# The PEER expert mixer of a two-layer decoder step: gathered expert rows replaced by a dense pass over all 16384 experts

## The chip, the cores and the metric

One Trainium2 chip (trn2), one core. The metric is the device time of one execution in microseconds; the median of three runs is the number that counts. The profile is that of one execution, taken by the hardware profiler.

## The reference

One inference step for 256 prompt tokens and 8 sample tokens (264 columns in all), D = 1024, everything in float32. Layer 0 mixes by a gated linear recurrence, layer 1 by latent attention over a paged cache; both layers end in the same expert mixer, which is what the change is about:

```python
q = (xb @ w_q).reshape(blk, PEER_HEADS, PEER_KEY_DIM)            # 8 heads
s1 = einsum('thd,hnd->thn', q[..., :half], k1)                   # 128 keys each
s2 = einsum('thd,hnd->thn', q[..., half:], k2)
v1, i1 = top_k(s1, 16); v2, i2 = top_k(s2, 16)
sv, si = top_k(all 256 sums v1 + v2, 16)
e = 128 * i1 + i2 at si                                          # of 16384 experts
gate = softmax(sv)
act = gelu(einsum('thkd,td->thk', u[e], xb), approximate=False)
y = einsum('thk,thkd->td', gate * act, v[e])
```

u and v are tables of 16384 x 1024 for each layer (67 MB each). Then x = LayerNorm(alpha * x + y).

## The kernel before, in words

Five engine programs are written out by hand and meet through semaphores (TensorE `pe`, ScalarE `act`, VectorE `dve`, GpSimd `pool`, and SyncE `sp`, which only issues transfers). The tokens lie in three tiles: two of 128 prompt tokens and one of 8 samples. `xT` holds x transposed, 8 blocks of 128 x 264. The program runs in stages: the recurrence (`*_hgrn`, 8 heads, `project` on L327 with 32 matmuls of 128 x 264 per head), join and normalisation (`pe_join` L646, `dve_ln` L670 to L685), the first mixer, attention (`*_mla`: prompt first, then the paged cache of each sample), join and normalisation, the second mixer, a last normalisation.

The mixer (`sp_peer`, `pool_peer`, `pe_peer`, `act_peer`, `dve_parts`) loops over the 8 heads, two per pass. For a head, TensorE computes the queries of all tokens (L919) and the scores (L927). VectorE chooses 16 of each half list and 16 of the 256 sums (`top16`, L1050 to L1060), looks up the indices by one-hot products over 16 x 16 (L1088 to L1092) and writes them to `idx`. POOL then gathers, for each tile and each of the 16 choices, one row of u per token into an eight-slot ring (L817, 512 KB), and the same of v. VectorE takes the dot product of every gathered u row with x (L1125, 512 in all); ScalarE applies Gelu and turns each column of weights into a 128 x 128 diagonal (L1021); TensorE multiplies it with the gathered v rows, so that they add up in PSUM (L944):

```python
for k in ks:
    after(pe, "pe", v_land[k % RING], 16 * (4 * hg + 2 * t + k // RING + 1))
    after(pe, "pe", dg_ready, 32 * hg + 16 * t + k + 1)
    for c in range(2):
        mm = pe.matmul(ybank(t, c, P), dg[:, k % 4, :], vring[:, k % RING, 512 * c:512 * c + 512], ...)
    mm.then_inc(v_free, 1)
```

The 8 samples are repacked so that their 128 choices fill one gather each of u and v (`repack` L935, `unpack_s`, L982). L944 therefore runs 2 layers x 8 heads x 2 tiles x 16 choices x 2 halves times. A head's routing runs one head ahead. The first head's routing of each layer is done apart and early (`pe_first`, `act_first`, L875 to L897): in layer 1, two of its three tiles lie inside attention, ahead of the page loop. In the first mixer a normalised tile is handed on while the next still adds up (L971, L977).

What the prediction also touches: `level_decays` (L474, L475) runs on VectorE and POOL at the same time, and L487 is a product of 1024 elements on POOL; L516 is a VectorE product with a pointer scalar; L1001 is ScalarE's copy of 264 columns out of PSUM; L1322 is the first matmul of attention.

## Time and profile before

| | |
|---|---|
| median of three runs | 2455.47 us (2450.78 to 2457.2) |
| span of the profiled execution | 2712.4 us, the only time shown for it |
| TensorE busy, matmul | 1916.9 us (71%), 6209 records |
| TensorE weight loads | 989.2 us, beside the matmuls |
| VectorE busy | 1398.3 us (52%) |
| ScalarE busy | 572.2 us (21%) |
| POOL busy | 1216.3 us (45%) |
| DMA | 642.5 MB, mean 237 GB/s |
| chain that ended last | PE 49%, issue 20%, VectorE 9% |

The span runs from the first to the last instruction of one profiled execution; it is 257 us longer than the median of the runs without the profiler. Busy is the union of an engine's instructions in the span. The granted clock is the share of TensorE's full 2.4 GHz; its other level is half of that, 1.2 GHz, and a mean between them says for how much of a stretch each held. A window row has its stretch and length first, then the busy time (and the number of records) of TensorE's matmuls, its weight loads, VectorE, ScalarE and POOL, then the clock, the DMA engines' busy share and GB/s.

### The profile page before, as it was taken

To read this page: it belongs to the slowest core of one execution; us is meant where nothing else is said; L and a number is where in the kernel's file an instruction comes from. 1 tells how busy PE (TensorE), PEld (TensorE's weight loads), DVE (VectorE), ACT (ScalarE), POOL (GpSimd) and SP (SyncE) were. 2 spreads that over 40 slices of the span, in tenths; PEclk is the share of its full clock that TensorE was granted. 3 is DMA by queue.
4 is the path that set the end of the run, shared out by engine and by line. 5 is a ranking of instruction groups with operands and counts; after the bars stand their busy time and mean duration, and the time that the engine had idled before them with its cause. 6 is when DMAs were issued, how large, how long until landed. Compare 5 with 4: busy or idle time off the path is not lost.

```text
span 2712.4 us, 28807 instructions
## 1 busy us (share of the span) xinstructions
PE 1916.9 (71%) x6209; PEld 989.2 (36%) x6209; DVE 1398.3 (52%) x3767; ACT 572.2 (21%) x1295; POOL 1216.3 (45%) x1229
## 2 busy tenths in 40 slices
PE   6997877556573847558887899877657484656657
PEld 5775343223332323223454444334223232223222
DVE  3554475664565656463252422347646555645563
ACT  3343021112121211122231333112212121111212
POOL 1110055764654657565002132435655465646464
PEclk9988878787786969779998999879778797877779
DMA  7530198996968869697303132468987788969596
GB/s 222 133 97 27 54 336 302 328 347 243 347 250 299 310 250 348 252 367 269 153 11 96 31 88 72 162 222 300 347 326 254 275 296 319 356 222 360 213 344 247
DMA packets 254991, 642.53 MB, mean 237 GB/s; under 512 B 23401, under 2 KB 115074, under 8 KB 254610
## 3 DMA queue, kind: packets, MB, share of 16 engines
q0 software_dynamic: 156160, 555.82, 56.1%
q1 hardware_dynamic: 98706, 85.37, 10.4%
q8 instruction: 38, 0.62, 0.1%
q14 instruction: 87, 0.71, 0.1%
HBM read 635.00 MB, written 6.10 MB: 236 GB/s over the span
## 4 chain that ended last, share of the span: by engine, by line
PE 49%; issue 20%; DVE 9%; another core or an unknown queue 7%; DMA 4%; ACT 4%; DVEq 3%; POOL 2%; PEldq 0%; ACTq 0%; SPq 0%; POOLq 0%; PEld 0%
PE bank L944 26%; DMA arena<-in_peer_v,idx 3%; PE bank L646 3%; PE bank L1447 2%; PE bank L1468 2%; POOL arena L817 2%; PE bank L919 2%; PE bank L338 1%; DVEq L476 1%; PE bank L327 1%; DMA arena<-in_peer_u,idx 1%; PE bank L1322 1%; PE bank L927 1%; PE bank L1349 1%
## 5 line engine op out<-in xcount | busy, mean ns | idle before, releaser
L944 PE MATMUL bank<-arena,dg 128*128 128x512 f32 x2048 | 974.8, 636 | 291.3 <-ACT dg L1021 153.9
L1125 DVE SCALAR_TENSOR_TENSOR arena<-arena,x 128x1024 f32<-128x1024 f32 x512 | 616.6, 1225 | 361.3 <-DMA arena<-in_peer_u,idx 323.7
L817 POOL DMA_INDIRECT arena<-in_peer_v,idx x512 | 531.1, 1037 | 597.2 <-DVE arena L1125 244.9
L944 PEld LDWEIGHTS bank<-arena,dg 128*128 128x128 f32 x2048 | 410.7, 205 | 843.1 <-issue 842.8
L817 POOL DMA_INDIRECT arena<-in_peer_u,idx x512 | 553.3, 1081 | 320.5 <-issue 260.3
L1021 ACT ACTIVATE dg<-cst,w 128x128 f32<-128x128 f32 x512 | 194.6, 399 | 759.6 <-PE bank L944 475.9
L919 PE MATMUL bank<-xT,wbig 128*128 128x264 f32 x448 | 116.7, 422 | 110.2 <-issue 110.2
L1311 POOL DMA_DIRECT2D arena<-in_cache_kpe x80 | 42.8, 536 | 275.9 <-issue 275.9
L919 PEld LDWEIGHTS bank<-xT,wbig 128*128 128x128 f32 x448 | 92.7, 211 | 129.9 <-issue 112.7
L927 PE MATMUL bank<-g_all 128*128 128x128 f32 (+1 forms) x168 | 36.6, 381 | 132.5 <-issue 106.6
L1104 DVE RECIPROCAL gsum_s<-gsum_s 8x1 f32<-8x1 f32 x16 | 2.4, 151 | 235.1 <-ACT rp L1010 207.0
L327 PE MATMUL bank<-xT,arena 128*128 128x264 f32 x512 | 117.0, 390 | 2.0 <-DMA arena<-in_hgrn_w_in 2.0
L327 PEld LDWEIGHTS bank<-xT,arena 128*128 128x128 f32 x512 | 97.8, 192 | 18.7 <-issue 2.0
L474 POOL TENSOR_TENSOR scratch<-scratch 128x128 f32<-128x128 f32 x16 | 7.0, 439 | 200.1 <-DVEq L523 200.1
L646 PE MATMUL bank<-wbig,xT 128*128 128x512 f32 (+1 forms) x192 | 91.0, 630 | 0.0
L935 PE MATMUL bank<-rp,cst 8*128 8x32 f32 x32 | 8.8, 362 | 114.2 <-DVE rp L1106 64.2
L927 PEld LDWEIGHTS bank<-g_all 128*128 128x128 f32 (+1 forms) x168 | 26.2, 223 | 142.7 <-issue 140.9
L1447 PE MATMUL bank<-arena,qst 128*16 128x512 f32 x128 | 60.4, 594 | 9.9 <-DVEq L1722 9.5
L1736 DVE COPY scratch<-bank 16x512 f32<-16x512 f32 x32 | 21.7, 679 | 85.6 <-PE bank L1448 85.4
L998 ACT ACTIVATE g_all<-bank 128x256 f32<-128x256 f32 x14 | 5.4, 383 | 242.4 <-remote 123.4
L1311 POOL DMA_DIRECT2D scratch<-in_cache_kpe x48 | 25.6, 534 | 66.8 <-issue 66.8
L646 PEld LDWEIGHTS bank<-wbig,xT 128*128 128x128 f32 (+1 forms) x192 | 31.4, 165 | 60.3 <-issue 60.3
(317 smaller groups left out, 2271.6 us busy)
## 6 DMA issues: line engine op xcount, KB each, us to landing
arena<-in_hgrn_w_in SPq DMA_DIRECT2D x32, 512.0 KB, 7.0
wbig<-in_peer_w_q SPq DMA_DIRECT2D x14, 1024.0 KB
arena<-in_cache_ckv SPq DMA_DIRECT2D x80, 128.0 KB, 2.0
arena<-in_peer_u,idx POOLq DMA_INDIRECT x512
arena<-in_peer_v,idx POOLq DMA_INDIRECT x512
scratch<-in_cache_ckv SPq DMA_DIRECT2D x48, 128.0 KB, 2.0
arena<-in_state_hgrn SPq DMA_DIRECT2D x8, 512.0 KB, 7.1
wbig<-in_hgrn_w_out SPq DMA_DIRECT2D x1, 4096.0 KB, 15.6
```

The lines of the kernel that those rows point to most:

```text
L327: mm = pe.matmul(bank[g % 2][:, 0:NT], wh[j][:, k, c, :], xT[:, k, :], start=(k == 0), stop=(k == KO - 1))
L338: mm = pe.matmul(bank[4 + l // 2][:, (l % 2) * 256 + t * P:(l % 2) * 256 + (t + 1) * P], left, right, start=True, stop=True)
L646: mm = pe.matmul(ybank(t, c, nt), xT[:, k, t0:t0 + nt], wbig[:, k, cols], start=False, stop=(k == KO - 1))
L817: pool.indirect_dma_start(out=dst, out_offset=None, in_=table, in_offset=bass.IndirectOffsetOnAxis(ap=rows, axis=0)).then_inc(done, 16)
L919: mm = pe.matmul(b[:, 0:NT], wq[j][:, k, s * P:(s + 1) * P], xT[:, k, :], start=(k == 0), stop=(k == KO - 1))
L927: mm = pe.matmul(b[0:nt, s * P:(s + 1) * P], qT[:, s, t0:t0 + nt], kT[:, s, :], start=True, stop=True)
L944: mm = pe.matmul(ybank(t, c, P), dg[:, k % 4, :], vring[:, k % RING, 512 * c:512 * c + 512], start=False, stop=False, skip_group_check=True)
L1021: act.activation(dg[:, k % 4, :], ident, ACT.Copy, scale=w[t][:, k:k + 1]).then_inc(dg_ready, 1)
L1125: dve.scalar_tensor_tensor(uring[:, k % RING, :], uring[:, k % RING, :], 1.0, x[:, t, :], ALU.mult, ALU.mult, accum_out=dots[t][:, k:k + 1 ...
L1311: eng.dma_start(buf[(b + 1) % 3][:, bass.ds(g, 1), :].rearrange("p a l -> p (a l)"), cache[page]).then_inc(landed[(b + 1) % 3], 16)
L1447: pe.matmul(out, qst[:, c, :], cT[:, q % 2, c, :], start=(c == 0), stop=False)
L1468: pe.matmul(out, dpT[:, pg, :], cbuf[slot][:, pg, :], start=(pg == 0), stop=False)
```

## The change

The gathers go. Each mixer streams its tables once, in tiles of 128 x 1024 (512 KB) through a ring of six: 16 tiles of w_q, 128 of u, 128 of v (`NSTREAM` = 272). The host lays the tables out so that a tile is contiguous. The program is unrolled.

- Queries: tile n of w_q against `xT` gives half a head's queries for all 264 tokens (`project`); scores follow for each head; those of the samples of all heads are computed at once from zero-padded queries (`zq`).
- VectorE does all routing of the layer in one go (`choose`, `indices`, `gates`): 8 heads for tile 0, then for tile 1, then the 64 rows of the samples. The results are a first key, a second key and a gate for every choice; TensorE turns them (`turn_table`) so that `tab` has choices on the partitions and tokens on the columns.
- Dense u: tile i (first key i, 128 second keys) against `xT`: 8 matmuls of 128 x 264 give the dots of 128 experts with all tokens. ScalarE writes their Gelu to row block H[:, i, :], 264 columns. H fills `big` (128 x 264 x 4 bytes on each partition), which also holds the former `scratch`, `arena` and `wbig`; the routing's buffers lie where rows 70 and above go.
- Gate map: from tile 62 (`FRONT`) on, each tile comes with one chunk of 4 tokens, 66 chunks in all. For a token, `hot2` (one-hot of the second key: POOL squares the distance, ScalarE takes relu(1 - d)) times `hot1` (one-hot of the first key times the gate, VectorE) sums the 128 choices to a 128 x 128 map of gates. VectorE multiplies it into the rows of H that are there (`use_gates`), ScalarE stores the others (`keep_gates`), and each later tile is multiplied in when its Gelu is ready (`gate_tile`).
- Dense v: tile i against H[:, i, :], 8 matmuls of 128 x 264, one for each PSUM bank, summed over all 128 tiles. VectorE adds alpha * xT, and TensorE turns the sum back for the normalisation, all three tiles after the last v tile.
- In attention, the first routings between the joins and the page loop go; `rt`, `qlT`, `olT`, `dpT` move into `shared`. Attention's weights w_dkv, w_dq, w_uq and w_ukv are loaded within the first layer's v tiles.

The diff, cut to its core:

```diff
-RING = 8
+RING = 6
+NSTREAM = 2 * HH + 2 * NKEYS
+NCHUNK = NT // 4
+FRONT = 62
+LAG = 1
+NTMP = NKEYS - (FRONT - LAG)
+TAB_AT = (56, 61)
...
+        big = sb("big", [P, NKEYS * NT])
+        scratch = big[:, 0:SCRATCH]
+        arena = big[:, SCRATCH:SCRATCH + 16384]
+        wbig = big[:, SCRATCH + 16384:].rearrange("p (k n) -> p k n", k=KO)
...
+        H = big[:, :].rearrange("p (i t) -> p i t", t=NT)
...
-            def gather(dst, table, rows, done):
-                pool.indirect_dma_start(out=dst, out_offset=None, in_=table,
-                                        in_offset=bass.IndirectOffsetOnAxis(ap=rows, axis=0)).then_inc(done, 16)
...
+            def stream(n):
+                m = NSTREAM * l + n
+                if m >= RING:
+                    sp.wait_ge(tile_done, m - RING + 1)
+                if n < 2 * HH:
+                    src = peer_w_q[l, n]
+                elif n < NA:
+                    src = peer_u[l, n - 2 * HH]
+                else:
+                    src = peer_v[l, n - NA]
+                dst = ring[:, m % RING, :]
+                if n < NA:
+                    dst = dst.rearrange("p (k n) -> p k n", k=KO)
+                sp.dma_start(dst, src).then_inc(land[m % RING], 16)
...
+            def project(n):
+                w = landed(n)
+                if n >= 4:
+                    pe.wait_ge(dps_taken, NA * l + n - 3)
+                for k in range(KO):
+                    mm = pe.matmul(bank[n % 4][:, 0:NT], w[:, k * P:(k + 1) * P], xT[:, k, :],
+                                   start=(k == 0), stop=(k == KO - 1))
+                mm.then_inc(tile_done, 1)
...
+            def gate_map(c):
+                if c == 0:
+                    pe.wait_ge(sc_ready, (HH + 1) * (l + 1))
+                    pe.wait_ge(tab_ready, 3 * (l + 1))
+                if c >= 4:
+                    pe.wait_ge(gate_kept, NCHUNK * l + c - 3)
+                pe.wait_ge(hot2_ready, NCHUNK * l + c + 1)
+                pe.wait_ge(hot1_ready, NCHUNK * l + c + 1)
+                for j in range(4):
+                    mm = pe.matmul(bank[4 + c % 4][:, j * P:(j + 1) * P], hot2[c % 2][:, j, :], hot1[c % 2][:, j, :],
+                                   start=True, stop=True)
+                mm.then_inc(gate_ready, 1)
...
+            for i in range(NKEYS):
+                if i == TAB_AT[0]:
+                    turn_table(0)
+                if i == TAB_AT[1]:
+                    turn_table(1)
+                if i == FRONT:
+                    turn_table(2)
+                if i >= FRONT:
+                    gate_map(i - FRONT)
+                project(2 * HH + i)
+                if i == 1:
+                    scores(HH - 1)
+                    sample_scores()
+            pe.wait_ge(gate_used, NCHUNK * (l + 1))
+            pe.wait_ge(gate_kept, NCHUNK * (l + 1))
+            for i in range(NKEYS):
+                w = landed(NA + i)
+                if i == FRONT - LAG:
+                    pe.wait_ge(tile_gated, NTMP * (l + 1))
+                for k in (4, 5, 6, 7, 0, 1, 2, 3):
+                    if i == 0 and k == 0:
+                        pe.wait_ge(dps_taken, NA * (l + 1))
+                    mm = pe.matmul(bank[k][:, 0:NT], w[:, k * P:(k + 1) * P], H[:, i, :],
+                                   start=(i == 0), stop=(i == NKEYS - 1))
+                mm.then_inc(tile_done, 1)
...
+            def act_tile(i):
+                act.wait_ge(tile_done, NSTREAM * l + 2 * HH + i + 1)
+                b = bank[(2 * HH + i) % 4]
+                n, j = gated(i), i - (FRONT - LAG)
+                if n:
+                    if j >= 3:
+                        act.wait_ge(tile_gated, NTMP * l + j - 2)
+                    ins = act.activation(tmp[j % 3][:, 0:n], b[:, 0:n], ACT.Gelu)
+                if n < NT:
+                    ins = act.activation(H[:, i, n:NT], b[:, n:NT], ACT.Gelu)
+                ins.then_inc(dps_taken, 1)
...
+            for c in range(NCHUNK):
+                keep_gates(c)
+                if c + 2 < NCHUNK:
+                    make_hot2(c + 2)
+                act_tile(FRONT + c)
...
+            for c in range(NCHUNK):
+                pool.wait_ge(tab_ready, 3 * l + chunk_tile(c) + 1)
+                if c >= 2:
+                    pool.wait_ge(hot2_ready, NCHUNK * l + c - 1)
+                d = dist[c % 2]
+                pool.tensor_tensor(d, bc(places, 1, 4), bc(tab[:, 1, 4 * c:4 * c + 4], 2, P), ALU.subtract)
+                pool.drain()
+                pool.tensor_tensor(d, d, d, ALU.mult).then_inc(dist_ready, 1)
...
+            def make_hot1(c):
+                dve.wait_ge(tab_ready, 3 * l + chunk_tile(c) + 1)
+                if c >= 2:
+                    dve.wait_ge(gate_ready, NCHUNK * l + c - 1)
+                for j in range(4):
+                    t = 4 * c + j
+                    ins = dve.tensor_scalar(hot1[c % 2][:, j, :], places, tab[:, 0, t:t + 1], tab[:, 2, t:t + 1],
+                                            ALU.is_equal, ALU.mult)
+                ins.then_inc(hot1_ready, 1)
...
+            def use_gates(c):
+                f = FRONT - LAG + c
+                dve.wait_ge(gate_ready, NCHUNK * l + c + 1)
+                dve.wait_ge(dps_taken, NA * l + 2 * HH + f)
+                h = H[:, 0:f, 4 * c:4 * c + 4].rearrange("p i t -> p t i")
+                dve.tensor_tensor(h, h, bank[4 + c % 4][:, :].rearrange("p (t i) -> p t i", t=4)[:, :, 0:f],
+                                  ALU.mult).then_inc(gate_used, 1)
+
+            def gate_tile(i):
+                n, j = gated(i), i - (FRONT - LAG)
+                dve.wait_ge(dps_taken, NA * l + 2 * HH + i + 1)
+                dve.wait_ge(gate_kept, NCHUNK * l + n // 4)
+                dve.tensor_tensor(H[:, i, 0:n], H[:, i, 0:n], tmp[j % 3][:, 0:n], ALU.mult).then_inc(tile_gated, 1)
...
+            make_hot1(0)
+            make_hot1(1)
+            for c in range(NCHUNK):
+                use_gates(c)
+                if c + 2 < NCHUNK:
+                    make_hot1(c + 2)
+                if c:
+                    gate_tile(FRONT - LAG + c - 1)
+            gate_tile(NKEYS - 2)
+            gate_tile(NKEYS - 1)
+            for k in range(KO):
+                dve.wait_ge(tile_done, NSTREAM * (l + 1))
+                dve.scalar_tensor_tensor(xT[:, k, :], xT[:, k, :], ALPHA, bank[k][:, 0:NT],
+                                         ALU.mult, ALU.add).then_inc(acc_taken, 1)
```

What moves on the engines. TensorE (`ring` is the stream's ring, `big` holds H and the routing's buffers, `arena` the gathered rows, `dg` the diagonals, `rp` the samples' choices), at the start of the first mixer, before:

```order
L944 MATMUL bank<-arena,dg 128x512 x16
L935 MATMUL bank<-rp,cst 128x32
L944 MATMUL bank<-arena,dg 128x512 x16
L914 MATMUL bank<-cst,wbig 128x128 x2
L919 MATMUL bank<-xT,wbig 128x264 x16
L927 MATMUL bank<-g_all 128x128 x4
L927 MATMUL bank<-g_all 8x128 x2
L944 MATMUL bank<-arena,dg 128x512 x32
L982 MATMUL bank<-wbig,wmask 8x512 x2
```

and now, from the samples' scores to the first chunk of the gate map:

```order
L827 MATMUL bank<-kT,big 64x128 x16
L806 MATMUL bank<-xT,ring 128x264 x432
L836 MATMUL bank<-cst,big 128x128 x3
L806 MATMUL bank<-xT,ring 128x264 x40
L836 MATMUL bank<-cst,big 128x128 x3
L806 MATMUL bank<-xT,ring 128x264 x8
L838 MATMUL bank<-cst,big 128x8 x3
L850 MATMUL bank<-x 128x128 x4
L806 MATMUL bank<-xT,ring 128x264 x8
```

The 512-column products with diagonals are gone, and runs of 264-column products stand in their place, eight to a tile; behind L838 the pair L850 and L806 repeats 66 times, and L882 follows with 1024 of them in one run.

VectorE in the chunk phase now (`shared` holds the turned table and three Gelu tiles, `x` the one-hots, `bank` the gate map):

```order
L1068 TENSOR_TENSOR big<-big,bank 128x4x66
L1059 TENSOR_SCALAR x<-cst,shared 128x128 x4
L1075 TENSOR_TENSOR big<-big,shared 128x20
L1068 TENSOR_TENSOR big<-big,bank 128x4x67
L1059 TENSOR_SCALAR x<-cst,shared 128x128 x4
```

In each chunk the product with the map grows by one row of H, the four one-hots stay, and the tile's own product grows by 4 columns up to 264; the dot products of 1024 elements that stood here before are gone.

## Rows read from the trace of the kernel before

**Rows 1.** The page: the span and the bytes
```profile
span 2712.4 us, 28807 instructions
...
HBM read 635.00 MB, written 6.10 MB: 236 GB/s over the span
```

**Rows 2.** Windows: busy PE, PEld, DVE, ACT, POOL; granted clock, DMA share, GB/s
```profile
0.00:337.00 337.00, 275.87 (x1275) 201.32 (x1276) 166.50 (x476) 101.84 (x213) 32.30 (x49) 0.89 0.38 105
337.00:1285.00 948.00, 610.47 (x1503) 289.89 (x1501) 541.40 (x1437) 170.21 (x415) 557.09 (x525) 0.80 0.83 305
...
1293.00:1773.00 480.00, 419.33 (x1974) 212.37 (x1974) 167.35 (x463) 129.91 (x254) 96.95 (x152) 0.94 0.28 91
1773.00:2701.00 928.00, 605.80 (x1442) 284.14 (x1442) 507.59 (x1362) 168.46 (x408) 530.01 (x504) 0.81 0.81 295
...
575.00:595.00 20.00, 12.28 (x38) 6.00 (x36) 16.67 (x27) 0.19 (x1) 15.43 (x16) 0.90 1.01 403
1600.00:1680.00 80.00, 75.91 (x382) 32.20 (x381) 20.90 (x60) 28.14 (x45) 24.05 (x45) 1.00 0.30 85
103.00:117.00 14.00, 14.00 (x65) 11.98 (x64) 10.97 (x30) 7.09 (x13) 3.62 (x5) 1.00 0.39 92
```

**Rows 3.** Groups of instructions: TensorE's matmuls on L944 and L327
```profile
L944 PE MATMUL bank<-arena,dg 128*128 128x512 f32 x2048 | 974.8, 636 | 291.3 <-ACT dg L1021 153.9 <-issue 111.0 <-DMA arena<-in_peer_v,idx 26.2
L327 PE MATMUL bank<-xT,arena 128*128 128x264 f32 x512 | 117.0, 390 | 2.0 <-DMA arena<-in_hgrn_w_in 2.0
```

**Rows 4.** Timeline of TensorE in a recurrence head: start us, us, instructions merged
```profile
101.22 1.95 PE L338 MATMUL bank<-scratch 128*128 128x128 f32 x16
103.01 14.41 PE L327 MATMUL bank<-xT,arena 128*128 128x264 f32 x64
```

**Rows 5.** Timeline: TensorE and VectorE as the first mixer starts
```profile
314.75 0.66 PE L875 MATMUL bank<-cst,keys_first 128*128 128x128 f32 x2 [2.41 <-ACT xT L631]
...
322.10 0.66 PE L623 MATMUL bank<-cst,o_all 8*128 8x8 f32 x8 [0.47 <-ACT g_all L897]
...
340.76 1.28 DVE L670 BATCH_NORM_STATS2 stats<-bank 8x6 f32<-8x512 f32 x2 [8.91 <-issue]
```

**Rows 6.** Timeline of VectorE: normalisations behind the first mixer
```profile
1285.66 1.30 DVE L670 BATCH_NORM_STATS2 stats<-bank 128x6 f32<-128x512 f32 x2 [3.27 <-PEq L977]
...
1290.30 1.28 DVE L670 BATCH_NORM_STATS2 stats<-bank 8x6 f32<-8x512 f32 x2
```

**Rows 7.** Timeline of TensorE in attention: the second mixer's first routings
```profile
1491.77 0.51 PE L875 MATMUL bank<-cst,keys_first 128*128 128x128 f32 x2 [2.52 <-ACT xT L631]
...
1505.46 0.71 PE L883 MATMUL bank<-g_all 128*128 128x128 f32 x4 [0.47 <-ACT g_all L893]
```

**Rows 8.** Timeline of VectorE over one choice of 16; groups by form
```profile
322.19 0.49 DVE L1050 MAX8 v<-g_all 128x8 f32<-128x128 f32 x2 [6.14 <-ACT g_all L897]
...
327.88 0.42 DVE L1060 FIND_INDEX8 si<-sv,cand 128x8 uint32<-128x256 f32 x1
...
L1090 DVE TENSOR_TENSOR oh<-oh,i12f 128x512 f32<-128x512 f32 x32 | 22.2, 692 | 2.4
...
L593 DVE TENSOR_TENSOR o_all<-o_all,rstd 128x1024 f32<-128x1024 f32 x2 | 2.5, 1226 | 0.2
```

**Rows 9.** Timeline of VectorE and of POOL in the first head
```profile
30.06 0.28 DVE L475 TENSOR_TENSOR scratch<-scratch 128x128 f32<-128x128 f32 x1
30.27 1.98 DVE L474 TENSOR_TENSOR scratch<-scratch 128x128 f32<-128x128 f32 x1
...
29.15 0.44 POOL L475 TENSOR_TENSOR scratch<-scratch 128x128 f32<-128x128 f32 x1
30.12 1.98 POOL L487 TENSOR_TENSOR arena<-arena,scratch 128x1024 f32<-128x1024 f32 x1 [0.53 <-issue]
```

**Rows 10.** Groups by form: a VectorE and a ScalarE instruction over 264 columns
```profile
L516 DVE TENSOR_SCALAR arena<-arena,omlb 128x264 f32<-128x264 f32 x8 | 2.9, 358 | 15.1 <-ACT arena L412 12.5 <-issue 2.6
...
L1001 ACT ACTIVATE g_all<-bank 128x264 f32<-128x264 f32 x28 | 10.4, 389 | 194.2 <-remote 151.9 <-PE bank L919 32.0 <-issue 10.3
```

More of the change, by code:

```diff
@@ L1055, in top16 @@
                 dve.drain()
-                for v_, i_, src, tmp in rows:
-                    dve.max(v_[:, 8:16], tmp)
+                for v_, i_, src, rest in rows:
+                    dve.max(v_[:, 8:16], rest)
                 dve.drain()
-                for v_, i_, src, tmp in rows:
-                    dve.max_index(i_[:, 8:16], v_[:, 8:16], tmp)
-            def route(hg, t, j, first=False):
-                nt = TILES[t][1]
-                after(dve, "dve", rs_taken, 6 * hg + (2 * t + 2 if first else 4 + t))
-                top16(*[(v12[0:nt, s, :], i12[0:nt, s, :], sc[0:nt, t, s, :], sc2[0:nt, s, :]) for s in range(2)])
+                for v_, i_, src, rest in rows:
+                    dve.max_index(i_[:, 8:16], v_[:, 8:16], rest)
@@ new lines, in dve_peer @@
+            NR = NS * HH
+            for h in range(HH):
+                dve.wait_ge(sc_ready, (HH + 1) * l + h + 1)
+                choose(h, P, sc[:, 0, h, :])
+            differences(P, HH, gex[0])
+            indices(P, HH, picked[0][:, 0:2, :].rearrange("p s (h k) -> p (s h) k", h=HH))
+            for h in range(HH):
+                choose(h, P, sc[:, 1, h, :])
+            gates(0, P, HH, gex[0], picked[0][:, 2, :].rearrange("p (h k) -> p h k", h=HH))
+            dve.sem_inc(picked_ready, 1)
@@ L1292, in sp_mla, with load_pages @@
             sp_ln(sp, 2)
-            load_pages(sp, cbuf, cache_ckv, page_in, lambda: sp_first(sp, 1))
-        def load_pages(eng, buf, cache, landed, between=None):
+            load_pages(sp, cbuf, cache_ckv, page_in)
+        def load_pages(eng, buf, cache, landed):
             eng.wait_ge(ptab_in, 16)
@@ L1301, in load_pages @@
             for b in range(NS):
-                if b == 2 and between:
-                    between()
                 if b == 1:
@@ L1728, in dve_mla @@
             dve_ln(dve, 2, (0, 1))
-            route, dot, weigh, heads = dve_parts(dve, 1)
-            for t in range(2):
-                route(HH, t, 0, True)
             def take_scores(b, q):
```

704 lines of the change are left out of this document (265 added, 439 removed).

## The prediction

> **What bounds the kernel now.** I read the stretches first, then the costliest groups, then the timeline at the borders of the two expert mixers. The stretches [rows 2] divide the span of 2712.4 us [rows 1]: 337 us of recurrence and joins, the first mixer up to 1285, attention from 1293 to 1773, the second mixer up to 2701, and a tail of 11. So the mixers hold 948 + 928 = 1876 us. In both the DMA share is above 0.8 at about 300 GB/s, TensorE is busy for only two thirds, and its granted clock is 0.80 and 0.81 of the full one. A stretch of gathers alone reaches 403 GB/s at share 1.01 [rows 2]. The mixers are paced by gathered rows, and in the gaps TensorE falls to its lower level of 1.2 GHz.
>
> The decisive row is of another kind. The program has 2 x 8 x 2 x 16 x 2 = 1024 matmuls on L944, and the trace has 2048 [rows 3]; it has 256 on L327, and the trace has 512. **An f32 matmul is two records**, and its cost is twice the step from one record to the next. That step stands in an unbroken run of L327 with just the shape that the change uses, 128x128 weights against 264 columns: 64 records, 14.41 us, the last lasting 0.386, so (14.41 - 0.39) / 63 = 0.2225 us at clock 1.00 [rows 2, 4]. One such matmul costs 0.445 us. For 128 columns the step is (1.95 - 0.27) / 15 = 0.112 us, a matmul 0.224 [rows 4].
>
> **The sum, part by part.**
> A tile of the stream (512 KB) feeds 8 matmuls of 264 columns: 3.56 us. A mixer has 16 tiles of w_q, 128 of u and 128 of v: 272 x 3.56 = 968.3 us. The one-hot products are 66 chunks x 4 matmuls x 0.224 = 59.1 us. Key scores: 32 matmuls, 7.2 us, and 16 for the samples, 3.6 us. Three turned tables, about 1.3. At the first chunk TensorE must wait for the last table to go through ScalarE (0.3) and to become a one-hot (0.6), about 1.5; the cold start costs about 2. Together **1043 us per mixer** where 948 and 928 stand now.
>
> What else runs in these 1043 us should hide behind TensorE:
> - Transfers: 512 KB in 3.56 us is 147 GB/s against 403 reached [rows 2], with five tiles in flight, 17.8 us of lead. The 7 MB of attention weights that SP now puts into the v tiles fit in the same margin. Without that cover the stream would cost 524 KB / 403 GB/s = 1.3 us per tile.
> - Routing on VectorE: one choice of 16 from two lists takes from 322.19 to 328.30, 6.1 us [rows 8]; 17 of them, 104 us. The index look-up for 8 heads has three passes over 4096 elements; from 512 and 1024 elements (0.69 and 1.23 us, 1.04 ns each more) a pass is 4.4 us, with its small operations 15 us, twice. With gates and samples and a start at 16 us it ends near 157 us. The third table is due at tile 78, after 78 x 3.56 + 11 = 289 us. There are 130 us to spare.
> - ScalarE: one or two Gelu reads per tile, 0.39 us each [rows 10]; in the chunk phase a 512-element one-hot and the kept gates besides, about 1.6 us of 4.46.
> - The chunk phase is the tight one. TensorE needs 3.56 + 0.90 = 4.46 us per chunk. VectorE: a product over 244 to 504 elements (0.42 to 0.69), four TENSOR_SCALAR of 128 (each at most the 0.36 of 264 columns), a product of up to 264 (0.42): 2.4 us. POOL: two products of 512 elements; between 0.44 for 128 and 1.98 for 1024 [rows 9] that is 1.1 each, 2.2 us. Side by side nothing is late. In turns they make 4.6 us, 0.1 above TensorE.
>
> What is removed: all gathers, the 512 dot products of 1.2 us, the diagonals, the per-head routing. None of it lies on the new path, so it is not subtracted again; it is the 1876 us that I replace. POOL's queue loses its gathers, and SP's queue only gains transfers with room around them.
>
> The rest moves little:
> - Start of the first mixer: TensorE no longer inserts the first routing at 314.75. The sample tile's turn and join, 322.10 to 340.76 (18.7 us) [rows 5], begin at about 313.5, end at 332, and with the normalisation (4.6, the distance of two BATCH_NORM rows [rows 6]) and the turn the mixer starts at **338**.
> - End of a mixer: now the tiles are normalised while others still accumulate. Later all come at once: eight reads of the sum 3, transposes 1, three normalisations 13.7, a turn 1: **18.5 us** before L1322 may start; at the very end **20** with the output.
> - Attention: 1293 to 1773, less the two first routings between 1490 and 1506 [rows 7], 15 us: **465**.
>
> Sum against the profile: 338 + 1043 + 18.5 + 465 + 1043 + 20 = **2927 us**, against the span of 2712.4.
>
> The runs of before have a median of 2455.5 us, 257 less than this profiled span. So profiling lengthens something, and no row says what. The TensorE part cannot shrink: 264 columns at 0.2225 us are the full 2.4 GHz with two cycles per column. I let only the other 842 us shrink: by nothing at one end, at the other by the whole 9.5% (80 us). Since the excess most likely sits in the transfer-bound mixers, which are gone, I take 4%, 32 us. That gives **2895 us** for a run, 18% slower.
>
> **Rules weighed.** POOL and VectorE do hinder each other: beside POOL's 1024-element product of 1.98 us a VectorE product of 128 elements took 1.98 instead of 0.28 [rows 9]. The Trainium skill (SBUF — State Buffer, Who interferes with whom) says the same: the shared port pair is an exclusive lock, and a VectorE instruction with two SBUF inputs, or in a two-port mode, waits for the whole GpSimd instruction. By that rule the chunk is the 4.6 us in turns, and my sum would be 2 x 66 x 0.14 = 18 us longer.
> The widest stride of a row here is 8 elements (no cost seen); the change reads H at a stride of 264. The same page (the note on cachelines in The DMA port swizzle) says that each access which crosses into a new 16-byte line pays a penalty, without a figure.
>
> **The rivals.**
> A. *The tile costs half, and the smaller traffic wins.* If a matmul were one record of 0.2225 us, a mixer would be 272 x 1.78 + 36 (half of the 71 us of one-hots, scores and tables) + 7 for starts and waits = 527 us were nothing else late. The chunk phase would then be paced by POOL and VectorE, up to 4.6 us for each of the 66 chunks in place of 2.2, so 527 to 680, and the run 810 + 2 x (527 to 680), 1865 to 2170: faster. For it: DMA is the bound now, and bytes fall from 635 MB [rows 1] to about 360. Against it: both counts in rows 3. The point from which it decides: 440 us lie between 2895 and 2455, over 2 x 2176 matmuls 0.10 each, so from 0.34 us per matmul downwards. Chance 0.03.
> B. *The chunk phase is bound by VectorE and POOL.* If strided products cost double (+0.5) and each locked operation loses a hand-over (five of 0.1), the chunk is 5.6 us, 1.1 above TensorE: 132 x 1.1 = 150 us, a run of 3045. It decides as soon as the two in turns pass 4.46 us. Chance 0.10.
> C. *Profiling lengthens everything alike.* 2927 x 0.905 = 2650 us. Against it: the full-clock step in rows 4. Still slower. Chance 0.06.
> D. *The clock does not hold for a millisecond of dense work.* From 1600 to 1680 TensorE was busy for 95% with clock 1.00 [rows 2], and the lower level appears here behind waits. Each per cent is 21 us; above 3100. Chance 0.03.
>
> **How the numbers follow.** Forecast as argued, 2820 to 2970: 0.77. A 0.03, B 0.10, C 0.06, D 0.03, and 0.01 for landing within 0.3% of before by a mix of A and the rest. The range takes the forecast's bounds (842 us shrunk by 80 at the low end, rounding the unknown ends down to 2820; the lock's 18 us and half of B at the high end): 2820 to 3000. A measurement can tell 0.3%, 7 us, from no change. Faster 0.03, same 0.01, slower 0.96.
>
> **What would show it.** Right: two records per matmul on the new lines of 264 columns, a step of 0.2225, granted clock 1.00 through both mixers, TensorE busy above 95% there, DMA near 150 GB/s, two mixers of about 1043 us. In the chunk phase TensorE's waits on the one-hots near zero. Wrong: gaps of TensorE behind VectorE or POOL of over 0.5 us per chunk (B), a clock below 0.95 in the dense tiles (D), tiles of 1.8 us (A), or a run more than 100 us below its own profile (C).

## The result and the profile after

The changed kernel takes **2930.9 us** (median of 4 runs, 2927.8 to 2931.6) against 2456.3 us of the kernel before (four runs, 2450.8 to 2468.1): ratio 1.193, interval 1.189 to 1.197, slower. Its profiled run took 2927.84 us with a span of 2926.2, so here profile and runs agree within 0.2%. One thing has to be known for all that follows: the kernel before takes 2451 to 2468 us on some chips and 2617 to 2722 on others, as the experiments show; where a ratio stands, it is against runs of the kernel before on that experiment's own chip, and since these scatter by 3% on the slower kind, a ratio there moves by 1% with the runs that it is taken against.

The page of the changed kernel, its busy times, slices, transfers and the chain that ended last (they answer to [rows 1] and to the page's chain of before):

```profile
span 2926.2 us, 36735 instructions
PE 2778.4 (95%) x13193; PEld 2205.2 (75%) x13193; DVE 851.2 (29%) x2583; ACT 512.6 (18%) x1231; POOL 381.1 (13%) x439
...
PE   7987999999999999999787998899999999999997
...
PEclk9987999999999999999898999999999999999999
...
DMA packets 160321, 357.89 MB, mean 122 GB/s; under 512 B 14473, under 2 KB 85666, under 8 KB 159666
...
PE 90%; DVE 3%; DVEq 2%; ACT 2%; issue 1%; SPq 0%; ACTq 0%; DMA 0%
```

Traffic fell from 643 to 358 MB and DMA is 0% of the chain; TensorE is 90% of it. The windows cut at the borders of the stages (first mixer, its tail, attention, second mixer, end, and the first mixer's chunk phase) answer to [rows 2]. The columns after the stretch are its length, then each engine's busy time, PEclk, DMA share and GB/s:

```profile
core 0: us, PE busy (x) PEld busy (x) DVE busy (x) ACT busy (x) POOL busy (x), PEclk, DMA share, GB/s
339.50:1383.30 1043.80, 1042.62 (x4988) 899.32 (x4988) 263.89 (x857) 139.72 (x380) 140.91 (x132) 1.00 0.47 143
1383.30:1399.20 15.90, 4.17 (x33) 3.24 (x33) 14.38 (x31) 1.84 (x5) 0.00 (x0) 0.79 0.80 284
1399.20:1863.90 464.70, 410.54 (x1900) 203.82 (x1900) 131.09 (x360) 127.91 (x248) 69.55 (x129) 0.94 0.18 51
1863.90:2906.60 1042.70, 1041.59 (x4988) 898.68 (x4988) 263.85 (x856) 139.70 (x380) 140.58 (x132) 1.00 0.45 136
2906.60:2926.20 19.60, 3.07 (x25) 2.38 (x24) 15.74 (x32) 0.88 (x3) 0.00 (x0) 0.71 0.14 55
633.40:923.70 290.30, 290.30 (x1567) 256.52 (x1568) 134.22 (x385) 89.42 (x259) 136.41 (x128) 1.00 0.39 118
```

TensorE is busy for 1042.6 of 1043.8 us of the first mixer, at clock 1.00. The chunk phase from the first to the last one-hot product has no gap at all, with VectorE at 134 and POOL at 136 of 290 us. So the time is the number of TensorE's records times their step. The groups of that chunk phase, busy time and mean of one, then idle time before them and its releaser:

```profile
L806 PE MATMUL bank<-xT,ring 128*128 128x264 f32 x1040 | 242.2, 386 | 0.0
L1059 DVE TENSOR_SCALAR x<-cst,shared 128x128 f32<-128x128 f32 x256 | 72.6, 347 | 0.0
L988 POOL TENSOR_TENSOR x<-cst,shared 128x512 f32<-128x512 f32 x64 | 70.0, 1094 | 149.9 <-ACT x L940 149.9
L850 PE MATMUL bank<-x 128*128 128x128 f32 x527 | 69.5, 275 | 1.1 <-ACT x L940 1.1
L990 POOL TENSOR_TENSOR x<-x 128x512 f32<-128x512 f32 x64 | 66.6, 1041 | 9.1
L1068 DVE TENSOR_TENSOR big<-big,bank 128x244 f32<-128x244 f32 (+32 forms) x65 | 54.3, 835 | 164.3 <-PE bank L850 164.3
```

L850 has waited 1.1 us in 66 chunks. The two lines of 264-column products over the whole run, and the v tiles of the first mixer in one piece of TensorE's timeline (start, length, records):

```profile
L806 PE MATMUL bank<-xT,ring 128*128 128x264 f32 x4608 | 1055.1, 387 | 0.6 <-ACT xT L624 0.6
L882 PE MATMUL bank<-big,ring 128*128 128x264 f32 x4096 | 911.7, 386 | 0.0
...
927.39 455.84 PE L882 MATMUL bank<-big,ring 128*128 128x264 f32 x2048
```

These are two records for each of the 2304 and 2048 products of the program, and the step from one record to the next is (455.84 - 0.39) / 2047 = 0.2225 us.

Where the time went: outside the mixers 339.5 + 15.9 + 464.7 + 19.6 = 840 us are left, about as before. The two mixers took 1876 us in the profile before and take 2086.5 now. A run of before of 2455 us leaves about 2455 - 840 = 1615 us for its mixers, 470 less than now.

### The profile page after: what moved, and what is told of

It is laid out like the page before. It is cut to its first block, busy times and chain, and to the rows that moved or that the text cites. A ratio compares the mean times of both kernels' runs of the same rounds, so it can differ in the third digit from the quotient of the medians.

```text
span 2926.2 us, 36735 instructions
## 1 busy us (share of the span) xinstructions
PE 2778.4 (95%) x13193; PEld 2205.2 (75%) x13193; DVE 851.2 (29%) x2583; ACT 512.6 (18%) x1231; POOL 381.1 (13%) x439
## 4 chain that ended last, share of the span: by engine, by line
PE 90%; DVE 3%; DVEq 2%; ACT 2%; issue 1%; SPq 0%; ACTq 0%; DMA 0%
PE bank L806 35%; PE bank L882 31%; PE bank L850 4%; PE bank L639 3%; PE bank L1380 2%; PE bank L1401 2%; PE bank L331 1%; DVEq L469 1%; PE bank L1381 1%; PE bank L320 1%; PE bank L1255 1%; PE bank L1282 1%; PE bank L1370 1%; PE bank L383 1%; PE bank L637 1%
## 5 line engine op out<-in xcount | busy, mean ns | idle before, releaser
L806 PE MATMUL bank<-xT,ring 128*128 128x264 f32 x4608 | 1055.1, 387 | 0.6 <-ACT xT L624 0.6
L806 PEld LDWEIGHTS bank<-xT,ring 128*128 128x128 f32 x4608 | 866.4, 191 | 142.0 <-ACT xT L624 0.8
L882 PE MATMUL bank<-big,ring 128*128 128x264 f32 x4096 | 911.7, 386 | 0.0
L882 PEld LDWEIGHTS bank<-big,ring 128*128 128x128 f32 x4096 | 778.2, 190 | 133.1
L1112 DVE SCALAR_TENSOR_TENSOR xT<-xT,bank 128x264 f32<-128x264 f32 x16 | 5.6, 421 | 909.6 <-PE bank L882 909.6
L988 POOL TENSOR_TENSOR x<-cst,shared 128x512 f32<-128x512 f32 x132 | 144.1, 1092 | 916.9 <-ACT shared L921 619.3
L1068 DVE TENSOR_TENSOR big<-big,bank 128x244 f32<-128x244 f32 (+21 forms) x132 | 110.8, 839 | 334.7 <-PE bank L850 334.7
L1059 DVE TENSOR_SCALAR x<-cst,shared 128x128 f32<-128x128 f32 x528 | 149.6, 347 | 0.2
L850 PEld LDWEIGHTS bank<-x 128*128 128x128 f32 x1056 | 138.5, 191 | 10.8 <-issue 2.3
L850 PE MATMUL bank<-x 128*128 128x128 f32 x1056 | 139.3, 275 | 2.2 <-ACT x L940 2.2
L990 POOL TENSOR_TENSOR x<-x 128x512 f32<-128x512 f32 x132 | 137.6, 1043 | 21.4 <-issue 2.8
L320 PE MATMUL bank<-xT,big 128*128 128x264 f32 x512 | 117.0, 390 | 1.8 <-DMA big<-in_hgrn_w_in 1.8
L320 PEld LDWEIGHTS bank<-xT,big 128*128 128x128 f32 x512 | 97.8, 192 | 18.5 <-issue 1.9
L940 ACT ACTIVATE x<-x,cst 128x512 f32<-128x512 f32 x132 | 91.7, 696 | 0.0
```

The source lines that it names most:

```text
L320: mm = pe.matmul(bank[g % 2][:, 0:NT], wh[j][:, k, c, :], xT[:, k, :], start=(k == 0), stop=(k == KO - 1))
L806: mm = pe.matmul(bank[n % 4][:, 0:NT], w[:, k * P:(k + 1) * P], xT[:, k, :], start=(k == 0), stop=(k == KO - 1))
L850: mm = pe.matmul(bank[4 + c % 4][:, j * P:(j + 1) * P], hot2[c % 2][:, j, :], hot1[c % 2][:, j, :], start=True, stop=True)
L882: mm = pe.matmul(bank[k][:, 0:NT], w[:, k * P:(k + 1) * P], H[:, i, :], start=(i == 0), stop=(i == NKEYS - 1))
L940: act.activation(hot2[c % 2], dist[c % 2], ACT.Relu, scale=-1.0, bias=ones[:, 0:1]).then_inc(hot2_ready, 1)
L988: pool.tensor_tensor(d, bc(places, 1, 4), bc(tab[:, 1, 4 * c:4 * c + 4], 2, P), ALU.subtract)
```

## The experiments

**Which kernel depends on the chip.** The prediction had found 257 us between the profile of the kernel before and its runs. The changed kernel was run again, unaltered, on a chip where before took 2628 to 2716 us.

> The changed kernel, unaltered, beside a run of the kernel before on the same chip. In the last group the kernel before took 2617 to 2693 us, not 2455. Theory A, the gathers of the kernel before depend on the chip or the placement, and the streaming kernel does not: 2928 to 2932 again, within 0.3%, while the kernel before is far from 2455. Theory B, the whole chip is slower: this one moves with it by 7%, above 3000.

2928.3 us (2927.3 to 2930.9), while before had a median of 2672 beside it. Theory A holds: the streaming kernel is the same within 0.1% on both chips, the kernel with gathers moved by 9% between the medians and by 7% between the fastest runs (2450.8 and 2627.8). Then the kernel before was profiled anew on that chip.

> The kernel before, unaltered, with a new profile beside unprofiled runs on the same chip. Two theories of the 257 us between its first profile (2712) and its runs (2455). Theory P, the profiler lengthens this kernel: its profile is again some 250 us above the runs of the same chip. Theory C, the chip does: on two chips the unprofiled runs took 2617 to 2716 us, on two others 2451 to 2468, so profile and runs agree within 2% here, near 2455 or near 2660 according to the chip; near 2455 the mixers hold about 820 us each instead of 948 and 928, with the stretches outside them unchanged.

Profiled 2718 us, the other runs 2655, 2704 and 2666, and seven more of the same kernel beside them 2651 to 2722: the profile lies within 2.4% of its own runs, inside the range of the others, and near the first profile's 2712. Theory P falls: no part of the 250 us that it asks for can be seen. So the first profile most likely came from a chip of the slower kind; which chip it was is not known. The windows of the new profile, mixer and attention, repeat [rows 2]:

```profile
337.00:1285.00 948.00, 618.88 (x1521) 293.27 (x1520) 549.63 (x1453) 172.43 (x419) 555.64 (x526) 0.81 0.84 307
1293.00:1773.00 480.00, 418.78 (x1977) 213.88 (x1975) 165.50 (x460) 129.60 (x253) 98.27 (x152) 0.93 0.27 82
```

No profile on a chip of the faster kind was taken of this kernel, so that its mixers hold the difference there stays inferred. For it speaks that the stretches outside the mixers add up to 840 us in the profile of the changed kernel, beside which before took 2456 us, and to 836 in the first profile of before. What the gathers have to do with it, the next run shows:

```diff
-                pool.indirect_dma_start(out=dst, out_offset=None, in_=table,
-                                        in_offset=bass.IndirectOffsetOnAxis(ap=rows, axis=0)).then_inc(done, 16)
+                pool.dma_start(dst, table[0:dst.shape[0], :]).then_inc(done, 16)
```

> The kernel before, with each gather of 128 rows by index replaced by a plain transfer of the same 512 KB (the first 128 rows of the table) from the same queue with the same waits; the rows are then not the chosen ones. Theory, the scattered rows or their descriptors pace the mixers: 555 MB at 403 GB/s are 1380 us over two mixers in place of about 1876, the run falls towards 2200 us and its spread to below 0.3%. Rival, another engine or the number of transfers in flight paces them: within 3% of the kernel before, with the same spread.

2378.6 us (2376.6 to 2379.9), ratio 0.889 (0.886 to 0.892) on that chip of the slower kind, or 0.90 against the two shortest runs of before there (2628 and 2656), and its spread is 0.14% instead of 3%. In its profile the first mixer ends at about 1130:

```profile
337.00:1130.00 793.00, 601.00 (x1519) 280.50 (x1517) 545.17 (x1450) 171.96 (x417) 277.76 (x524) 0.88 0.95 365
...
L817 POOL DMA_DIRECT2D arena<-in_peer_u x512 | 271.6, 530 | 368.8 <-DVE arena L1124 192.7
```

As many bytes move at 365 GB/s instead of 307. Time and spread both hang on fetching chosen rows. Whether it is where the rows lie, that the edit reads the same 128 rows each time, or the issue on POOL (a mean of 530 ns instead of 1071) these runs don't separate: the edit changes all three. The fall is also less than the 2200 expected: the transfers reach 365 GB/s at share 0.95, not the 403 that the expectation took. This kernel was not run on a chip of the faster kind.

**Is it TensorE's columns?** Four of eight products left out in the u and v tiles:

```diff
+KUSE = 4
+VUSE = (4, 5, 0, 1)
...
-                for k in range(KO):
+                ks = range(KO) if n < 2 * HH else range(KUSE)
+                for k in ks:
...
-                for k in (4, 5, 6, 7, 0, 1, 2, 3):
+                for k in ((4, 5, 6, 7, 0, 1, 2, 3) if i in (0, NKEYS - 1) else VUSE):
```

> Left out: 4 of the 8 products of each u tile and of each v tile but the first and last (the sums are then not the full ones); transfers, routing, gate maps stay. Theory 1, TensorE's columns set the time everywhere: a tile is 1.78 us instead of 3.56, a chunk 1.78 + 0.90 = 2.68, a mixer 57 + 110 + 11 + 177 + 231 = 586 us instead of 1043.7, the run 839 + 2 x 586 = 2011 us. Theory 2, VectorE and POOL work in turns in the chunk phase (2.1 + 2.2 = about 4.2 us per chunk, hidden so far under TensorE's 4.46): the same, but a chunk of 4.2, a mixer of 686 and a run of about 2211 us, with TensorE idle behind L1059 or L940 in the chunk phase alone. Theory 3, transfers set the time: almost no gain, above 2800.

2059.5 us (2056.7 to 2062.5), 871 less than the changed kernel, near theory 1 (2011) and far from 2 (2211) and 3. The windows of q and u tiles, chunk phase, and v tiles, then the groups of the chunk phase:

```profile
339.50:523.00 183.50, 182.44 (x861) 156.47 (x860) 128.16 (x467) 48.05 (x120) 4.63 (x4) 0.99 0.70 232
523.00:706.00 183.00, 176.26 (x1034) 154.51 (x1035) 181.52 (x380) 82.40 (x256) 137.79 (x128) 1.00 0.63 185
710.00:952.00 242.00, 235.01 (x1042) 199.22 (x1040) 0.76 (x2) 1.68 (x2) 0.00 (x0) 0.99 0.85 298
1803.80:2035.00 231.20, 231.20 (x1040) 197.42 (x1040) 0.73 (x2) 1.67 (x2) 0.00 (x0) 1.00 0.82 280
...
L1062 DVE TENSOR_SCALAR x<-cst,shared 128x128 f32<-128x128 f32 x256 | 123.2, 543 | 0.0
L853 PE MATMUL bank<-x 128*128 128x128 f32 x528 | 70.8, 277 | 7.5 <-DVE x L1062 6.2 <-ACT x L943 1.1
L993 POOL TENSOR_TENSOR x<-x 128x512 f32<-128x512 f32 x64 | 70.6, 1103 | 9.1
```

A chunk took 2.83 us (184 us over 65 steps) and not 4.2: VectorE and POOL do overlap. But VectorE is busy for 181.5 of 183 us: its TENSOR_SCALAR grew from 347 to 543 ns, so it now paces the chunk. And the first mixer's v tiles took 242 us where the second's took 231: in the first alone TensorE waits for v tiles, 7.0 us in all, and there alone the 7 MB of attention weights are loaded. Hidden in the changed kernel, they show once the stream itself asks for 280 GB/s.

With one product of eight left, everything under TensorE shows:

> Left out: 7 of the 8 products of each u tile and of each v tile but the first and last. Floors under TensorE: the v tiles come at the rate of the transfers, 524 KB at 403 GB/s = 1.3 us each, 167 us for 128; the tiles before the chunks end with the routing on VectorE, about 172 us after the start of the mixer; the chunk phase is 4.2 us per chunk if VectorE and POOL work in turns (277 us), 2.3 if side by side (152 us). A mixer of 616 us in turns, 491 side by side; the run about 2071 or 1821 us.

1919.5 us (one run), between the two sums. The same three stretches of its first mixer:

```profile
397.00:511.00 114.00, 81.53 (x228) 42.96 (x226) 100.16 (x343) 38.53 (x88) 10.91 (x5) 0.65 0.79 309
511.00:698.00 187.00, 114.52 (x649) 87.90 (x650) 185.00 (x379) 80.38 (x253) 137.80 (x128) 0.92 0.56 180
698.00:868.00 170.00, 134.43 (x257) 56.85 (x255) 4.77 (x12) 3.34 (x9) 0.00 (x0) 0.62 0.99 392
```

v tiles 170 us at 392 GB/s (expected 167); first chunk at 511, 171.5 us after the mixer's start (172); a chunk 2.9 us, VectorE busy for 185 of 187. These are the floors: 57 + 114 + 187 + 170 = 528 us per mixer, half of what TensorE makes of it.

**The room of the chunk phase.** More work for POOL, nothing is left out:

```diff
                 pool.tensor_tensor(d, bc(places, 1, 4), bc(tab[:, 1, 4 * c:4 * c + 4], 2, P), ALU.subtract)
                 pool.drain()
+                for _ in range(2):
+                    pool.tensor_tensor(d, bc(places, 1, 4), bc(tab[:, 1, 4 * c:4 * c + 4], 2, P), ALU.subtract)
+                    pool.drain()
```

The edit adds two products per chunk, not the one that the text below speaks of: POOL gets about 4.2 us per chunk instead of 3.3, and the sums there become 2931 side by side, if 4.2 and its pauses still fit, and 2.0 + 4.2 = 6.2 us per chunk, 1.74 above TensorE's 4.46, 132 times: about 3160, in turns.

> Nothing left out; POOL does its first product of 512 elements twice per chunk, 1.04 us more for 132 chunks. Side by side: POOL 3.3 us per chunk under TensorE's 4.46, no change, 2931. In turns with VectorE: 2.1 + 3.2 = 5.3 to 5.4 us per chunk, 0.9 above TensorE, 132 x 0.9 = 119 us, about 3050.

2948.4 us (2946.8 to 2949.8), 17 to 20 us more and far from 3160. The chunk is 4.58 us, 0.13 above the changed kernel's 4.45, and 132 x 0.13 = 17. Groups of the chunk phase of the first mixer:

```profile
L1062 DVE TENSOR_SCALAR x<-cst,shared 128x128 f32<-128x128 f32 x256 | 178.3, 756 | 0.0
L991 POOL TENSOR_TENSOR x<-cst,shared 128x512 f32<-128x512 f32 x128 | 136.7, 1068 | 18.2
...
L993 POOL TENSOR_TENSOR x<-x 128x512 f32<-128x512 f32 x64 | 69.3, 1083 | 9.1
L988 POOL TENSOR_TENSOR x<-cst,shared 128x512 f32<-128x512 f32 x64 | 66.4, 1038 | 13.4 <-ACT x L940 13.4
...
L1071 DVE TENSOR_TENSOR big<-big,bank 128x244 f32<-128x244 f32 (+32 forms) x66 | 55.7, 843 | 61.7 <-PE bank L850 61.7
```

POOL's products, (136.7 + 69.3 + 66.4) / 64 = 4.26 us per chunk with pauses between them, leave it hardly any wait (13.4 us in 64 chunks, none of it between 730 and 930 us). On TensorE's timeline the chunks come 4.45 us apart up to 729 us and 4.60 from there on: POOL itself now paces the chunk. Strict turns are refuted. What suffers is VectorE's TENSOR_SCALAR (347 to 756 ns, 1.6 us per chunk), while the product whose second operand lies in PSUM stays at 0.84. Two pieces of the changed kernel's own timeline show the same within one kernel: four TENSOR_SCALAR beside POOL's products, and four with POOL idle.

```profile
635.07 2.75 DVE L1059 TENSOR_SCALAR x<-cst,shared 128x128 f32<-128x128 f32 x4
635.46 1.04 POOL L988 TENSOR_TENSOR x<-cst,shared 128x512 f32<-128x512 f32 x1
...
800.12 1.10 DVE L1059 TENSOR_SCALAR x<-cst,shared 128x128 f32<-128x128 f32 x4
...
801.26 1.08 POOL L988 TENSOR_TENSOR x<-cst,shared 128x512 f32<-128x512 f32 x1 [2.20 <-ACT x L940]
```

After some chunks the two fall into turns by themselves, since POOL waits for L940, which waits for TensorE. That costs nothing while the turns fit into 4.45 us. The Trainium skill (SBUF — State Buffer, Who interferes with whom) says that instructions with at most one SBUF input outside the two-port modes do not contend, and that TENSOR_SCALAR can be in such a mode; the 843 ns beside the 756 agree.

Three of four one-hot products left out from the fifth chunk on (those tokens have stale gates):

```diff
-                for j in range(4):
+                for j in ((0, 1, 2, 3) if c < 4 else (0,)):
```

> Left out: 3 of the 4 one-hot products of each chunk from the fifth chunk on (those tokens then have stale gates). TensorE alone: 62 x 3 x 0.224 x 2 = 83 us less than the changed kernel's 2931, 2848 us, as VectorE's own floor of a chunk (2.8 us) is far below the 3.79 us that are left. Rival, the chunk waits for the chain through ScalarE and POOL: less than half of it, above 2890.

2845.6 us (one run), 83 to 85 less: these small products lie on the path at their full 0.224 us each (83 us for 372 of them).

**The cover of the transfers.** Fewer tiles in the ring, two or three instead of six:

```diff
-                if m >= RING:
-                    sp.wait_ge(tile_done, m - RING + 1)
+                if m >= LEAD:
+                    sp.wait_ge(tile_done, m - LEAD + 1)
```

> The changed kernel with two tiles in flight or in use instead of six: a transfer is issued when the tile two before it is done, so it has one tile of TensorE, 3.56 us, while one took 3.5 us from issue to landing. Theory, that landing time is a latency with one transfer in flight and holds: almost nothing is hidden beyond it, the wait after the semaphore adds some 0.1 to 0.4 us per tile, 544 tiles: 50 to 200 us, 2980 to 3130. Rival, a lone transfer lands in 1.3 + some latency, below 3 us: no change, 2931.

> Three tiles in flight or in use instead of six, so a transfer has 7.1 us. Both theories of lead_of_two: no change, within 0.3% of 2931; if it is longer, the cover by five tiles was needed and the transfers' share in the prediction was wrong.

3045.5 and 2931.8 us (one run each). With two, the 115 us are 0.21 per tile, as the first theory said; the wait stands at the tiles' first weights:

```profile
L883 PE MATMUL bank<-big,ring 128*128 128x264 f32 x2048 | 479.2, 392 | 24.8 <-DMA ring<-in_peer_v 23.2
...
L883 PEld LDWEIGHTS bank<-big,ring 128*128 128x128 f32 x2048 | 383.6, 191 | 120.3 <-DMA ring<-in_peer_v 58.3
```

Three tiles are enough; of the five tiles of lead, three are spare.

**What the products would cost with other operands.** The two records belong to f32. The v phase was turned to bf16 products: H is kept as bf16, and VectorE and ScalarE, idle there, cast the tiles in turn (these operands are rounded to bf16, the rest stays f32).

```diff
-                w = landed(NA + i)
+                pe.wait_ge(cast[i % 2], (NKEYS * l + i) // 2 + 1)
+                w = w16[i % 4]
...
+            if i % 2:
+                ins = eng.activation(w16[i % 4], ring[:, m % RING, :], ACT.Copy)
+            else:
+                ins = eng.tensor_copy(w16[i % 4], ring[:, m % RING, :])
```

> The second table's tiles are cast to bf16 by VectorE and ScalarE in turn (the engines are idle there), H is kept in bf16, and the products of the v phase are bf16 (so that part is computed with rounded operands). Theory: the price of the change is the two records of an f32 product; in bf16 a product of 264 columns is one record of 0.11 us, a tile 0.9 us, and the v phase goes at the rate of the transfers, 1.3 us per tile: 167 instead of 455.7 us, the run 2931 - 2 x 289 = 2354 us, below the kernel before. Rival: with TensorE busy for two thirds the clock falls to 0.5 as in the kernel before and a tile is 1.76 us, 225 us, 2470. Rival: transfers or casts (about 1.1 us each, two engines) are slower than 2 us per tile: above 2550.

2381.1 us (2380.5 to 2383.5), ratio 0.907 (0.902 to 0.913) against the shortest runs of before on that chip, near 2625 us (0.896 against their median of 2657), and 550 us under the changed kernel where 577 were expected. The v phase of its first mixer, groups from it, and the line over the whole run:

```profile
930.00:1108.00 178.00, 124.91 (x952) 89.27 (x952) 41.03 (x60) 61.65 (x60) 0.00 (x0) 0.92 1.00 383
...
L895 PE MATMUL bank<-big,x 128*128 128x264 bf16 x877 | 116.1, 290 | 51.3 <-ACT x L737 49.2 <-DVE x L739 2.0
L737 ACT ACTIVATE x<-ring 128x1024 bf16<-128x1024 f32 x55 | 58.1, 1056 | 110.2 <-DMA ring<-in_peer_v 108.8 <-PE bank L895 1.4
...
L895 PE MATMUL bank<-big,x 128*128 128x264 bf16 x2048 | 263.1, 284 | 98.3 <-ACT x L737 88.6
```

One record per product now (2048 records for 2 x 128 x 8), and the casts wait for the transfers: 178 us, 1.4 per tile, at DMA share 1.00. The clock fell a little (0.92), not to 0.5 throughout as the rival had it.

Then the u tiles as well, cast by ScalarE, with the turned x cast once:

```diff
+            def cast_u(i):
+                act.wait_ge(land[m % RING], 16 * (m // RING + 1))
+                act.activation(wu16[i % 4], ring[:, m % RING, :].rearrange("p (a n) -> p a n", a=4), ACT.Copy).then_inc(ucast, 1)
```

> As v_in_bf16, and the first table too: ScalarE casts each u tile and VectorE once the turned x; w_q, the keys and the one-hot products stay f32, so the routing of the first mixer is exact. Theory: the tiles before the chunks end with the routing, about 174 us after the start of the mixer; a chunk is VectorE's 2.8 us beside POOL (as with one product per tile), 187 us; the v phase 181 as in v_in_bf16; with starts and ends a mixer of 545 us, the run 839 + 1090 = 1929 us. Rival: ScalarE, with 1.06 for the cast, 0.7, 0.42 and 0.6 per chunk and its waits in order, becomes the bound of the chunk, 3.3 us or more: 1990 or above. Rival: the clock falls to 0.5 in the chunk phase and TensorE needs 1.8 + 1.8: 3.6 us, 2030.

1968.4 us (1965.8 to 1976.6), ratio 0.737 (0.734 to 0.740), or 0.745 against the two shortest runs of before there, 39 us above the expectation. The groups of its chunk phase name the reason, and a piece of its timeline gives the step of a bf16 product:

```profile
L1109 DVE TENSOR_TENSOR big<-big,bank 128x244 bf16<-128x244 bf16 (+32 forms) x65 | 115.3, 1773 | 3.7 <-PE bank L876 3.7
...
643.00 1.06 PE L832 MATMUL bank<-big 128*128 128x264 bf16 x8
```

Eight records in 1.06 us, the last of 0.28: 0.112 us each, a quarter of the f32 product's 0.445. The product on H takes 1.77 us where it took 0.84, and the chunk 3.10, both means over the phase (the expectation below says 1.82 and 3.2), where half_products had a chunk of 2.83. The casts of u are not the reason: v_in_bf16, whose chunk phase has bf16 rows of H and no casts, has 1.775 too. So H was left in f32 until the v phase, its rows cast then (`eng.tensor_copy(h16[i % 4], H[:, i, :])`), and the u casts moved into lnw.

> As both_tables_bf16, but H stays f32 until the v phase, where VectorE casts its rows too (u tiles are cast into lnw, the turned x has its own buffer). In both_tables_bf16 the chunk took 3.2 us and not 2.8, with the product on H at 1.82 us where it is 0.84 in the changed kernel. Theory, the strided access to bf16 elements of H is what costs: the product is 0.84 us again, the chunk 2.8, and the run 2 x 66 x 0.4 = 53 us shorter, about 1916. Rival, ScalarE's queue paces the chunk (its casts of 1.05 us were added in that kernel too): the product is 0.84 but the chunk stays at 3.2 and the run at 1965.

**1941.5 us** (1937.5 to 1946.5), ratio 0.790 (0.787 to 0.792) against before at 2459 on that chip: the fastest version that leaves nothing out, with both tables' products on rounded operands, 21% below the kernel before and 34% below the changed one. Against the 1968.4 of another chip it is 27 us less, half of the 53 expected. Its u tiles before the chunks, chunk phase and v phase, and two groups of the chunk phase:

```profile
399.00:512.50 113.50, 84.23 (x591) 59.32 (x590) 99.47 (x342) 94.96 (x150) 4.26 (x5) 0.94 0.83 308
512.50:702.50 190.00, 133.81 (x1056) 111.53 (x1056) 188.52 (x392) 142.57 (x327) 137.01 (x128) 0.99 0.61 184
702.50:879.00 176.50, 124.38 (x895) 85.43 (x896) 62.01 (x169) 57.69 (x56) 0.00 (x0) 0.91 0.98 374
...
L1105 DVE TENSOR_SCALAR x<-cst,shared 128x128 f32<-128x128 f32 x256 | 122.6, 538 | 0.0
L1114 DVE TENSOR_TENSOR big<-big,bank 128x244 f32<-128x244 f32 (+32 forms) x66 | 55.4, 839 | 3.1 <-PE bank L879 3.1
```

The product is 0.84 us again, so the strided bf16 access was its cost. The chunk is 2.85, the floor of VectorE beside POOL, and ScalarE with 143 of 190 us does not pace it. The 0.93 us by which the product is shorter are not all VectorE's time: the next instruction starts 1.32 us after a bf16 product of 360 elements begins and 0.75 us after an f32 one of 372, as the ends overlap. Of these 0.6 us the chunk keeps 0.25, and TENSOR_SCALAR takes back 0.30 (busy for 103.2 us before and 122.6 now, in 64 chunks). Each stage now has its own bound: routing, then VectorE, then transfers.

## Why the prediction came out right, and its wrong step

Term by term, in us:

| step | forecast | measured |
|---|---|---|
| start of the first mixer | 338 | 339.5 |
| a mixer | 1043 | 1043.8 and 1042.7 |
| tail before attention | 18.5 | 15.9 |
| attention | 465 | 464.7 |
| end | 20 | 19.6 |
| sum, against the profile | 2927 | 2926.2 |
| taken off for a run | 32 | 0 |

- **Two records per f32 product** was the decisive reading [rows 3], and the step [rows 4] held: 0.2225 us over the 2048 records of the v tiles. half_products took out 1016 products per mixer, 904 us at 0.445, and the run fell by 871, with VectorE pacing the chunks of what was left; bf16 products, one record of a quarter of the cost, turned the change to the faster side. Rival A needed a product below 0.34 us: v_in_bf16, with 1.4 us per v tile and 3.56 per other one, averages 0.32, and lies below 2455.
- **The wrong step** is "profiling lengthens something ... I take 4%, 32 us". It put the forecast at 2895, 36 us below the run (4% of the 842 us are 34, not 32; that changes nothing). For the changed kernel the profiled run and the others agree within 0.2%, and for the kernel before, on one chip, the profiled 2718 us lie within 2651 to 2722; the 257 us are the size of the difference between the two kinds of chip. The clue was in the shown numbers: a profile 10% above runs that scatter by 0.3%. That the excess belonged to mixers that are gone was a guess that fits all that was measured since, but it speaks for taking nothing off. The range held the run because these 32 us are small beside it, not because the term was right. Rival C (2650) rested on the same misreading.
- **The chunk phase.** VectorE was forecast with 2.4 us and takes 134.2 / 66 = 2.0, POOL 2.1 for 2.2. Inside it L1068 takes 0.60 to 1.08 us, mean 0.84, where 0.42 to 0.69 was forecast for 244 to 504 elements: the stride of 264 elements does cost, 0.2 to 0.4 us. At 264 elements the row itself takes 0.64 us, and L1112, 264 elements side by side and also with an operand in PSUM, 0.42. The TENSOR_SCALAR, forecast with at most 0.36, last 0.35 on average, and four of them alone take 1.10 us, a step of 0.28. "In turns 4.6, 0.1 above TensorE" did not come: the two alternate inside TensorE's time, and where they collide TENSOR_SCALAR is stretched. The 4.6 us had every VectorE instruction wait for POOL, the product with PSUM too, which does not. Rival B, 5.6 us per chunk, has no support: with one product of eight left the phase takes 2.9.
- **Covers.** Transfers: shown by lead_of_three (no change) and lead_of_two (115 us). Routing: forecast to end 157 us after the start with 130 to spare. VectorE's choices ended at 503.6, 164 us after it, and the look-up's passes took 4.42 us (4.4 forecast). But two rows of VectorE's timeline show what was missed:

```profile
608.04 0.29 DVE L1046 TENSOR_REDUCE big<-big 128x8 f32<-128x128 f32 x1 [104.41 <-ACT big L916]
...
619.66 0.55 DVE L1096 TENSOR_TENSOR big<-big,cst 64x384 f32<-64x384 f32 x1
```

It waits 104 us for the exponential, which ScalarE's order puts behind u tile 54, and has the third table at 620.2, 11 us before TensorE turns it (631.5). The slack exists, but the order on ScalarE spends it; nothing was late.
- **Clock** (rival D): 1.00 through both mixers.
- **Tail**: 2.6 us too long in the sum, because attention's first products (L1255, at 1399.2) start while the third tile is still being normalised.

## What to carry to other kernels

Before trading transfers for dense products, count records per product in the trace and multiply by the step in a full-clock run: here 285 MB less traffic did not pay for f32 products of 0.445 us each, while with bf16 operands at 0.112 the same plan is the faster one (the kernel before was not tried with bf16 operands, and no version here has its tables in bf16 in memory). Where a profile and the runs of the same kernel disagree by more than the runs' scatter, ask first whether they ran on the same chip. Then take TensorE's work away in one experiment: it shows in one profile what each stage falls back on.

## What the runs showed of the hardware

- The kernel that fetches scattered 4 KB rows differs between chips by 7% (fastest runs) to 9% (medians), and on the slower ones between runs by 3%; with as many bytes from the first 128 rows it scatters there by 0.14%, and the streaming kernel took 2927 to 2932 us on both kinds of chip.
- A VectorE product in place at a stride of 264 f32 elements costs 0.60 us for 244 elements and 1.08 for 504, against 0.42 for 264 elements (L1112) and 0.69 for 512 (L1090 of before) side by side. With the elements in bf16 (stride 528) it lasts 1.21 for 244 and 2.30 for 504, 1.77 on average, more than twice the f32 one.
- TENSOR_SCALAR of 128 f32 elements lasts 0.32 us at the least (a step of 0.28), 0.35 on average in the changed kernel, 0.54 where POOL and VectorE set the pace (half_products), and 0.76 with twice the products on POOL; a product with one operand in PSUM stays at 0.84 in all of these, and POOL's own stay at 1.04 to 1.10.
- TensorE busy for 70% of the v phase in bf16, with waits between the tiles, kept a granted clock of 0.91 to 0.92; with one f32 product per tile, busy for 134 of 170 us, it was 0.62.
